# Leaving out column sums that three stages do not read, and charging a planner for TensorE's changes of array shape

## The reference, cut to what matters

```python
def rms_norm(x, g):                       # ahead of each projection
    return x * rsqrt(mean(x*x, -1) + 1e-6) * g

def first_block(x, ...):
    proj = rms_norm(x, norm_mix) @ w_in
    ...                                   # two mixers
    x = x + mix @ w_out
    gate, up = split(rms_norm(x, norm_ffn) @ w_gate_up)
    return x + (silu(gate) * up) @ w_down

def second_block(x, ...):
    for l in range(2):                    # l = 0: diff_attention, l = 1: swa_sink_attention
        x = x + attention(rms_norm(x, attn_norm[l]))
        g, u = split(rms_norm(x, ffn_norm[l]) @ w_gate_up[l])
        x = x + (silu(g) * u) @ w_down[l]
    return x
```

## Time and profile before

| | |
|---|---|
| device time, median of 3 runs | 1882.84 us (1881.79 to 1883.13) |
| span of the profiled execution, first to last instruction | 1880.6 us |
| TensorE matmul busy | 1863.9 us, 99% of the span |
| VectorE busy | 1124.2 us, 60% |
| ScalarE busy | 778.9 us, 41% |
| GpSimd busy | 278.1 us, 15% |
| DMA moved | 166.52 MB, mean 89 GB/s |

### The profile page before, as it was taken

One profiled execution on the slowest core, in us unless ns is written; L12 is line 12 of the kernel. 1 busy time (PEld: TensorE's weight loads), 2 busy tenths in 40 slices (PEclk: granted clock), 3 DMA queues, 4 the chain that ended last, 5 costly groups with the idle time before them and its releaser, 6 DMA issues.

```text
span 1880.6 us, 24035 instructions
## 1 busy us (share of the span) xinstructions
PE 1863.9 (99%) x9258; PEld 1490.0 (79%) x9258; DVE 1124.2 (60%) x1782; ACT 778.9 (41%) x1728; POOL 278.1 (15%) x217
## 2 busy tenths in 40 slices
PE   9999999999999999999999999999999999999999
PEld 6887777888888888777688888888866788888887
DVE  7555885754454465588875445445978765445343
ACT  6435776332232232476643223223357533223221
POOL 2000551211010121111021101101210111011010
PEclk9999999999999999999999999999999999999999
DMA  6231000333333233322133332332332123333333
GB/s 230 59 104 63 24 2 20 93 101 96 95 101 93 98 90 101 102 78 77 48 102 92 99 101 92 99 101 82 104 107 63 62 90 101 95 96 101 92 94 95
DMA packets 51536, 166.52 MB, mean 89 GB/s; under 512 B 6880, under 2 KB 7264, under 8 KB 51168
## 3 DMA queue, kind: packets, MB, share of 16 engines
q1 hardware_dynamic: 51424, 165.00, 28.7%
HBM read 155.01 MB, written 2.10 MB: 84 GB/s over the span
## 4 chain that ended last, share of the span: by engine, by line
PE 91%; DVE 6%; ACT 1%; issue 1%; DMA 1%; SPq 1%; POOL 0%; DVEq 0%; ACTq 0%
PE bank L987 25%; PE bank L989 25%; PE bank L988 24%; PE bank L1097 2%; PE bank L1157 2%; PE bank L961 2%; PE bank L962 2%; PE bank L963 2%; DVE WL L1622 1%; PE bank L1010 1%; PE bank L1187 1%; PE bank L1199 1%; PE bank L1235 1%; PE bank L1212 1%; PE bank L1125 1%
## 5 line engine op out<-in xcount | busy, mean ns | idle before, releaser
L1302 ACT ACTIVATE WH<-RAW 128x512 fp32r<-128x512 f32 (+2 forms) x584 | 331.8, 613 | 772.0 <-PE bank L989 687.8
L1622 DVE TENSOR_TENSOR WL<-RAW,WH 128x512 fp32r<-128x512 f32 (+2 forms) x584 | 458.9, 822 | 75.7 <-ACT WH L1302 69.7
L987 PE MATMUL bank<-GH,WH 128*128 128x512 f32 x1088 | 433.1, 398 | 0.6 <-DVE GL L1908 0.6
L987 PE MATMUL bank<-HH,WH 128*128 128x512 f32 x1056 | 422.0, 400 | 2.4 <-DVE HL L1637 1.3
L989 PE MATMUL bank<-GH,WL 128*128 128x512 f32 x1088 | 423.9, 390 | 0.0
L988 PE MATMUL bank<-GL,WH 128*128 128x512 f32 x1088 | 423.6, 389 | 0.0
L989 PE MATMUL bank<-HH,WL 128*128 128x512 f32 x1056 | 411.6, 390 | 0.0
L988 PE MATMUL bank<-HL,WH 128*128 128x512 f32 x1056 | 411.3, 389 | 0.0
L2169 POOL TENSOR_TENSOR TMP<-TMP,RST 128x512 f32<-128x512 f32 x66 | 116.2, 1761 | 864.9 <-DVE TMP L2079 864.9
L987 PEld LDWEIGHTS bank<-GH,WH 128*128 128x128 f32 x1088 | 204.4, 188 | 45.2 <-issue 3.5
L988 PEld LDWEIGHTS bank<-GL,WH 128*128 128x128 f32 x1088 | 204.5, 188 | 43.1 <-issue 2.6
(11 more groups left out here) (252 smaller groups left out, 1889.7 us busy)
## 6 DMA issues: line engine op xcount, KB each, us to landing
RAW<-in_wgu SPq DMA_DIRECT2D x132, 512.0 KB, 3.5
RAW<-in_wd SPq DMA_DIRECT2D x48, 512.0 KB, 3.5
RAW<-in_wd SPq DMA_DIRECT2D x24, 384.0 KB, 3.1
RAW<-in_da_qk SPq DMA_DIRECT2D x16, 512.0 KB, 3.6
TMP<-TMP SPq DMA_DIRECT2D x104, 64.0 KB, 2.0
RAW<-in_w_inh SPq DMA_DIRECT2D x12, 512.0 KB, 3.7
RAW<-in_w_out SPq DMA_DIRECT2D x8, 512.0 KB, 3.7
RAW<-in_da_v SPq DMA_DIRECT2D x8, 512.0 KB, 3.5
```

The lines of the kernel that those rows point to most:

```text
L987: e.matmul(b, w_h, hi[st.x][k], start=(k == 0), stop=False)
L1302: e.activation(whs[s % NW][:, a:b], raw[s % NR][:, a:b], ACT.Copy).then_inc(S["wh"], 1)
L1622: e.tensor_tensor(wls[s % NR][:, a:b], raw[s % NR][:, a:b], whs[s % NW][:, a:b].bitcast(F), ALU.subtract).then_inc(S["wl"], 1)
```

## The change

What changes:

- `lz4` and `lz5a` exist only for even j. The semaphore counts that later steps wait for are lowered to match (`lz_c` from 3 to 2 and from 5 to 3, `lz_pe` and `lz_ln` to `j // 2 + 1`). GpSimd's first write to `ACC` in a later norm waits for `lz_a` of every norm and `lz_pe` of the even ones. In the plan, `nb` is given free for odd j by `lz2v`, and the feed-forward's first ScalarE step needs `lz3a` instead of `lz5a`.
- The planner gives each TensorE step a shape: "rows" (`sc`, `c_sc`), "cols" (`vl` of n and s) or "all". A step whose shape differs from the one before it ranks later by `TURN[old][1] + TURN[new][0]` ns, and lasts longer by the same amount.
- A token-major step of a unit needs in the plan the same step (t < 4) of the unit ahead of it.
- Beside the left-out steps and these counts no instruction changes its form; what else changes is the order.

```diff
+    TURN = {"rows": (60, 160), "cols": (140, 170), "all": (0, 0)}
+
+    @staticmethod
+    def shape(step):
+        if step[0] in ("sc", "c_sc"):
+            return "rows"
+        return "cols" if step[0] == "vl" and step[1] != "d" else "all"
...
-                rank = (first, due[step] if engine in engines else t, q[0][6])
+                turn = 0
+                if engine == "PE" and self.shape(step) != held:
+                    turn = self.TURN[held][1] + self.TURN[self.shape(step)][0]
+                rank = (first, (due[step] if engine in engines else t) + turn, q[0][6])
...
+            if engine == "PE":
+                ns, held = ns + best[3], self.shape(step)
...
-                          operand(name, k), k == 0 and bank_before(name, i), u > 0 and t == 4 * st.per - 1 and last[u - 1],
+                          operand(name, k), k == 0 and bank_before(name, i), ul and t < 4 and ("tri", name, u - 1, t), u > 0 and t == 4 * st.per - 1 and last[u - 1],
...
-        o.add("PE", ("lz1", j), 1500, ("pag", 8 * j + 7), j == 0 and ("cf_in",), take=("nb", ("lz5a", j)))
+        o.add("PE", ("lz1", j), 1500, ("pag", 8 * j + 7), j == 0 and ("cf_in",), take=("nb", ("lz2v" if j % 2 else "lz5a", j)))
         o.add("DVE", ("lz2v", j), 700, ("lz1", j), kind="lz2v", first=-1, lands=800)
-        o.add("PE", ("lz4", j), 1000, ("lz2v", j), kind="lz4", first=-1)
         o.add("ACT", ("lz3a", j), 1250, ("lz2v", j), first=-1)
-        o.add("ACT", ("lz5a", j), 450, ("lz4", j))
+        if j % 2 == 0:
+            o.add("PE", ("lz4", j), 1000, ("lz2v", j), kind="lz4", first=-1)
+            o.add("ACT", ("lz5a", j), 450, ("lz4", j))
...
-                o.add("ACT", ("e_gua", f, kk), 540, ("e_guv", f, part, 2 * k), ("lz5a", j))
+                o.add("ACT", ("e_gua", f, kk), 540, ("e_guv", f, part, 2 * k), ("lz3a", j))
...
-                norm_bank("lz_ln", j + 1)
+                norm_bank("lz_ln", j // 2 + 1)
...
-                b, r_ = token_rows("dv0" if j < 4 else "dv1", j % 4, 3)
+                b, r_ = token_rows("dv0" if j < 4 else "dv1", j % 4, 2)
...
-                b, r_ = token_rows("vs", i, 5)
+                b, r_ = token_rows("vs", i, 3)
...
-                p.wait_ge(S["lz_pe"], g // 8)
+                p.wait_ge(S["lz_a"], g // 8)
+                p.wait_ge(S["lz_pe"], (g // 8 + 1) // 2)
```

More of the change, by code:

```diff
@@ L145, in forwards @@
         self.ends, self.taken, self.given, self.begin, order = dict(self.end), {}, [], {}, []
-        events, unit, idle = list(self.ends.values()), 0, 0
+        events, unit, idle, held = list(self.ends.values()), 0, 0, "all"
         while len(order) < self.n:
@@ L158, in forwards @@
                     first = -1 if step[1] <= unit + 1 else 2
-                rank = (first, due[step] if engine in engines else t, q[0][6])
+                turn = 0
+                if engine == "PE" and self.shape(step) != held:
+                    turn = self.TURN[held][1] + self.TURN[self.shape(step)][0]
+                rank = (first, (due[step] if engine in engines else t) + turn, q[0][6])
                 if best is None or rank < best[0]:
-                    best = (rank, q, giver)
+                    best = (rank, q, giver, turn)
             if best is None:
@@ L1331, in lazy_column @@
                 c = LBT[:, 24:28]
-                p.wait_ge(S["lz_pe"], j + 1)
+                p.wait_ge(S["lz_pe"], j // 2 + 1)
                 e.activation(c, nb[:, 0:8:2], ACT.Ln, bias=eps, scale=1.0 / 1024).then_inc(S["lz_ln"], 1)
-                p.wait_ge(S["lz_ln"], j + 1)
+                p.wait_ge(S["lz_ln"], j // 2 + 1)
                 e.activation(c, c, ACT.Exp, scale=-0.5).then_inc(S["lz_c"], 1)
```

## The result

The changed kernel takes 1885.32 us (median of 20 runs, 1884.26 to 1886.26), the kernel before 1882.45 us on the same chip: ratio 1.0014, 95% interval [1.0007, 1.002]. It is slower by 2.9 us where 4.0 us less was forecast, and 0.8 us above the stated range. The span of its profiled execution is 1882.9 us against 1880.6.

The account below looks back on a forecast made before the run. TensorE, busy 99% of the span, was taken as the bound. Column sums -2.7, passages -0.3 and truer durations -1.0 made -4.0 us, a forecast median of 1878.8 us, range 1873.5 to 1884.5.

Parts of the forecast that it names:

- Column sums left out: Dropping `lz4` at j = 1, 3, 5 saves 0.90 us each on TensorE, 2.7 us in all.
- small-product rival: The dropped sums' small products were nearly free, so only 0.6 us goes: 1882.2 us, chance 0.03.
- Scale columns, waits, counts, dependency: Leaving out `lz5a`, the lowered counts and waits, and the order within token-major units: each taken as 0 on the path.
- Passages: TensorE's changes of shape: three new `vl` pairs, less 0.3 us for broken `vl`-score neighbours, win 0.3 us.
- class ranks decide nearly all choices: In d and s; argument for the rival of column sums only, order no better, 1880.1 us, chance 0.20.
- Truer durations: Planner's changed TensorE step times: -2.0 us in n/h, +1.0 in d and s together, -1.0 us in all.
- The slower rival: Scores and transposes of d and s stand too early on TensorE, 8 us of new waits: 1888 us, chance 0.10.
- The clock: TensorE's granted clock, full in every slice before, stays full after the change.

Follow-up runs that it names:

- rank_only: The changed kernel with TURN added to the planner's rank only, assumed durations as before: 1881.58 us, ratio 0.9994 to the kernel before.
- rows_only: The changed kernel with TURN kept for score steps alone, cols at (0, 0): 1881.29 us, ratio 0.9994 to the kernel before.
- cols_h400: The changed kernel with TURN for half-column steps alone, plus 400 ns assumed latency on each level product of the recurrence: 1883.81 us, ratio 1.0007.
- lag_195: The changed kernel with TURN at zero and LAG at 195 instead of 200 ns: 1883.74 us, ratio 1.0003 to the kernel before.
- measured: The changed kernel with TURN at zero and the trace's times assumed for score and `vl` steps: 1883.92 us, ratio 1.0006 to the kernel before.
- n_sc_220: The changed kernel with TURN at zero and 220 ns more assumed for each score step of n: 1883.64 us, ratio 0.9999.
- d_sc_440: The changed kernel with TURN at zero and 440 ns more assumed for each score step of d: 1883.28 us, ratio 1.0002.

## Why the prediction was wrong

- *Column sums left out:* right. Forecast 0.90 us for each, measured 0.9 to 1.0 in every kernel without them, and 24 records on the line. The small-product rival falls. Not foreseen: 0.4 to 1.0 us of the gains can be lost again at the s head, where the rope chain through DMA had no slack.
- *Scale columns, waits, counts, dependency:* right, nothing seen of them. The waits of `lz1` for GpSimd rose by 0.15 us at j = 3.
- *Passages:* the size was right by luck. I took three new pairs of `vl` steps and a loss of broken neighbours. No pair came, and `vl` ahead of a score went from four to six, worth 0.2 us by my own prices; I had 0.3. The reading that in d and s the turn changes no choice held for the rank in d (no step moved in `rank_only`) but not in s (68 of 252 steps), and with the assumed times 178 of 378 steps moved in d and 106 in s. So "class ranks decide nearly all choices" was wrong.
- *Truer durations:* the step that failed. I took -2.0 us in n/h and +1.0 in d and s together; the stretches show +2.3 in n/h and +1.3 and +1.9 in the others, so -1.0 became +5.5. The argument was that an assumed time nearer the truth gives a better order. The runs don't bear it out where it can be tested best: with the true times of the score and `vl` steps n/h takes 335.0 to 336.7 us against 332.4, and d 259.1 and 259.7 against 258.1, while a `LAG` 5 ns shorter costs 2.7 us in all by the medians. Only in s do the true times go with a better stretch. The order before was in n/h and d the shortest of those that ran, but for the doubt at `rows_only`. From such a place reorderings of 39 to 306 steps came out 0.3 to 4.3 us longer in n/h and 0.8 to 3.7 in d, the highest of each with the clock in it. My bounds of 10 us for this term were wide enough, but I put the value on the wrong side and the upper end of the range only 2 us above no change.
- *The slower rival,* "TensorE early at the tails", had the right sign; it was priced at 8 us of new waits, and the stretches grew by 5.5. Its mechanism is not shown. In d a score charge of 80 ns, which is true, gives 259.1 and 259.7 us, 220 ns gives 259.4 to 260.0 and 440 ns 260.3 to 262.0, so even a charge that isn't too long costs nearly as much. In n/h the waits sit at the recurrence as well as at its end.
- *The clock:* "stays full" was right for the changed kernel. That a new order can also lose by a fall of the clock behind its waits, up to 1.7 us each, was not in the sum at all; it showed in the experiments.
- Open: why a longer assumed step of n makes a worse n/h order. The late end of the recurrence goes with it: 3.3 to 7.1 us late in the seven orders with 334.3 us or more beside `cols_h400`, 0.8 to 1.4 late in the other four. Of those, three took 332.7 to 333.5 and `cols_h400` 336.6*. In s the order by true times is good twice, but so is one with false times.

## What to carry to other kernels

When a list scheduler writes the order of an engine that is busy 99%, a change of its cost numbers is close to a new draw of the order, and if the present order is the best of several, the draw is more likely to lose, also when the numbers get truer: this is the reading that fits n/h and d here, argued from 11 and 5 orders and not proven. Measure the spread first, with a change that means nothing, and freeze the order when the gain of another edit is to be read. Look at the granted clock of the very execution whose stretches you compare. Where stretches are separate in the plan, change one stretch at a time and keep each stretch's best: that gave 1878.97 us here, ratio 0.9981.

## What the runs showed of the hardware

The wait of 1.53 us at 229.53 ends a chain on VectorE. Its three products of 128x128 there (L2050, in the changed kernel), and GpSimd beside them:

```profile
225.42 2.77 DVE L2050 TENSOR_SCALAR HX<-HX,LBT 128x128 f32<-128x128 f32 x3
```

```profile
225.17 1.45 POOL L2171 TENSOR_TENSOR HX<-HX,P 128x512 f32<-128x512 f32 x1
226.59 0.84 POOL L2165 TENSOR_TENSOR HX<-HX,P 128x256 f32<-128x256 f32 x1
227.39 1.36 POOL L2156 TENSOR_TENSOR HX<-HX 128x256 f32<-128x256 f32 x2
```

```profile
L2050 DVE TENSOR_SCALAR HX<-HX,LBT x12: 270/338/1293, 225.4 to 295.2; 128x128 f32<-128x128 f32 x12
```

They take 2.77 us together where GpSimd runs all the time. Over the stretch the five that begin beside a GpSimd instruction take 0.68 to 1.29 us each, the seven others 0.27 to 0.34. This agrees with the Trainium skill ("SBUF — State Buffer", section "SBUF: two separate sides"): VectorE's two-port operations and GpSimd share a pair of ports under an exclusive lock. Who holds the ports is in no row. The planner doesn't model it, so here an order that brings the two together pays some 1.9 us (2.77 less three times 0.3). All twelve of these products, before and after:

```profile
L2036 DVE TENSOR_SCALAR HX<-HX,LBT 128x128 f32<-128x128 f32 x12 | 3.9, 376 | 0.0
L2050 DVE TENSOR_SCALAR HX<-HX,LBT 128x128 f32<-128x128 f32 x12 | 6.2, 570 | 0.0
```

They take 2.3 us more on VectorE. But `lag_195` has nearly the same (5.9 us) and its n/h is only 0.3 us longer, so more of this on VectorE doesn't by itself make the stretch longer; what counts is whether TensorE waits behind it, as it does at 229.53. How much of the 2.3 us in n/h is this was not tried.

The granted clock fell to 0.50 (1.2 GHz) for some 3.4 us seven times inside the attention stretches of these kernels. Each time it fell during or shortly behind a wait of TensorE: 1.05 and 0.99 us in `cols_h400`, 2.25 in `measured`, 1.60 in `n_sc_220`, 1.82 in `rows_only`, 1.04 in `d_sc_440`, 1.32 in `lag_195`. Not every such wait goes with a fall: the changed kernel waited 1.53 and 1.58 us with the clock full. So a wait can cost more than its own length.
